# The first MLP's first matrix product by seven products of half size, with its results kept in DRAM until the second product

## The reference, cut to what matters

```python
def _rmsnorm(x, gain):
    y = xf * lax.rsqrt(jnp.mean(xf * xf, axis=-1, keepdims=True) + NORM_EPS)
    return (y * gain).astype(x.dtype)

def _squared_relu_mlp(h, w1, w2):          # w1: 1024 x 4096, w2: 4096 x 1024
    a = jax.nn.relu(h @ w1)
    return (a * a) @ w2

x = x + mix                                # mix = o @ w_out
x = x + _squared_relu_mlp(_rmsnorm(x, norm_mlp[layer]), mlp_w1[layer], mlp_w2[layer])
```

## Time and profile before

| | |
|---|---|
| median of three runs | 2844.92 us (2844.15 to 2849.19) |
| the profiled execution | 2845.62 us, span of its instructions 2843.8 us |
| TensorE busy | 2764.9 us, 97% of the span |
| VectorE, ScalarE busy | 1307.6 us, 890.9 us |
| DMA | 213 MB, 75 GB/s over the span |

### The profile page before, as it was taken

One profiled execution on the slowest core, in us unless ns is written; L12 is line 12 of the kernel. 1 busy time (PEld: TensorE's weight loads), 2 busy tenths in 40 slices (PEclk: granted clock), 3 DMA queues, 4 the chain that ended last, 5 costly groups with the idle time before them and its releaser, 6 DMA issues.

```text
span 2843.8 us, 40766 instructions
## 1 busy us (share of the span) xinstructions
PE 2764.9 (97%) x17644; PEld 2306.9 (81%) x17644; DVE 1307.6 (46%) x1649; ACT 890.9 (31%) x1304; POOL 177.1 (6%) x153
## 2 busy tenths in 40 slices
PE   8999998999999999998899999999999999999999
PEld 7887887878888888886889778877777888888887
DVE  6445454455444544336525555565635333333332
ACT  5445444331221111226222443344423111221111
POOL 2212122100000000005100000000000000000000
PEclk9999999999999999999899999999999999999999
DMA  4111110314333342122323221121711111111111
GB/s 130 41 36 31 38 39 24 110 61 133 113 111 125 126 126 74 45 67 75 114 89 103 66 78 50 49 70 36 283 52 45 45 52 45 52 46 51 51 46 67
DMA packets 211267, 213.08 MB, mean 75 GB/s; under 512 B 6929, under 2 KB 186641, under 8 KB 211089
## 3 DMA queue, kind: packets, MB, share of 16 engines
q1 hardware_dynamic: 211088, 210.48, 23.3%
HBM read 188.44 MB, written 22.02 MB: 74 GB/s over the span
## 4 chain that ended last, share of the span: by engine, by line
PE 75%; DVE 3%; ACT 3%; issue 1%; POOL 1%; DMA 0%; ACTq 0%; POOLq 0%; DVEq 0%; SPq 0%
PE ps L415 10%; PE ps L418 10%; PE ps L431 10%; PE ps L688 8%; PE ps L681 8%; PE ps L679 8%; PE ps L874 2%; PE ps L875 2%; PE ps L879 2%; PE ps L501 2%; PE ps L497 2%; PE ps L499 2%; PE ps L849 1%; PE ps L828 1%; ACT Whi L1125 1%
## 5 line engine op out<-in xcount | busy, mean ns | idle before, releaser
L1589 DVE TENSOR_TENSOR Wlo<-Wraw,Whi 128x1024 fp32r<-128x1024 f32 x216 | 268.7, 1249 | 946.7 <-ACT Whi L1125 946.7
L1125 ACT ACTIVATE Whi<-Wraw 128x1024 fp32r<-128x1024 f32 x228 | 239.6, 1057 | 1251.7 <-PE ps L431 573.6
L415 PE MATMUL ps<-Hh,Whi 128*128 128x512 f32 x1408 | 437.2, 392 | 0.0
L418 PE MATMUL ps<-Hh,Wlo 128*128 128x512 f32 x1408 | 434.5, 390 | 0.0
L679 PE MATMUL ps<-ah,Whi 128*128 128x512 f32 x1024 | 398.8, 389 | 1.2 <-ACT ah L1302 1.2
L681 PE MATMUL ps<-ah,Wlo 128*128 128x512 f32 x1024 | 398.4, 389 | 0.0
L431 PE MATMUL ps<-Hl,Whi 128*128 128x512 f32 x1392 | 339.2, 393 | 0.0
L418 PEld LDWEIGHTS ps<-Hh,Wlo 128*128 128x128 f32 x1408 | 264.8, 188 | 55.5
L415 PEld LDWEIGHTS ps<-Hh,Whi 128*128 128x128 f32 x1408 | 262.6, 188 | 53.8
L431 PEld LDWEIGHTS ps<-Hl,Whi 128*128 128x128 f32 x1392 | 259.5, 188 | 56.5 <-issue 3.3
L688 PE MATMUL ps<-al,Whi 128*128 128x512 f32 x1024 | 253.4, 389 | 0.1
(11 more groups left out here) (309 smaller groups left out, 3626.9 us busy)
## 6 DMA issues: line engine op xcount, KB each, us to landing
Wraw<-in_m_w SPq DMA_DIRECT2D x128, 512.0 KB, 4.0
n<-in_w_ada SPq DMA_DIRECT2D x64, 512.0 KB, 3.5
Wraw<-in_w_in SPq DMA_DIRECT2D x56, 512.0 KB, 4.1
R<-in_xT SPq DMA_DIRECT2D x16, 512.0 KB, 4.9
Wraw<-in_w_gate SPq DMA_DIRECT2D x16, 512.0 KB, 4.2
gate_scratch<-gr SPq DMA_DIRECT2D x32, 256.0 KB, 2.4
Wraw<-in_w_out SPq DMA_DIRECT2D x8, 512.0 KB, 4.3
xs_scratch<-R SPq DMA_DIRECT2D x8, 512.0 KB, 3.0
```

The lines of the kernel that those rows point to most:

```text
L415: e.matmul(t[:, c], wh[:, k, ms], opd.hi[:, k, c], start=k == 0, stop=False)
L418: e.matmul(t[:, c], wl[:, k, ms], opd.hi[:, k, c], start=False, stop=False)
L1125: e.activation(Whi[n % 4][:], Wraw[n % 2][:], ACT.Copy).then_inc(*S("w_hi").tick(n))
L1589: e.tensor_tensor(Wlo[n % 4][:], Wraw[n % 2][:], Whi[n % 4][:].bitcast(F), ALU.subtract).then_inc(*S("w_lo", "v").tick(n))
```

## The change

The first product (hidden = w1 transposed x) is cut in two in each of its three dimensions and made by Strassen's scheme in seven products of half blocks instead of eight. The hidden tiles go in 16 pairs q; a product takes 128 hidden rows, 4 pieces of width and 512 tokens: 12 matmuls. VectorE makes the sums of weight blocks (`a_sum`) and, once, the sums of x blocks (`b_minus`); both are split into high and low (`a_part`, `b_part`). `SEQ` gives the order of the 112 products. Partial sums stay in PSUM while further products are added to them, and ScalarE copies them out between (`part_copy`); VectorE adds what the four quarters of a pair need (`quarter`).

The operand is x times the gain, without the norm's root; the root (`rstd`) multiplies the results after ReLU. The last output tile of w_out is made in another order, so that its operands' buffers come free piece by piece.

The results are squared by ScalarE, written to DRAM (`a_scratch`) in quarters of 256 KB and read back as tiles of 512 KB (`a_load`) to 14 pairs of buffers, then split (`a_split`). All 32 hidden tiles are made before the first chunk. During chunk i SyncE loads the four tiles of chunk i + 1, one at each odd output tile.

The dot products all move into the second product: ten in each of the chunks 0 to 6 until they are used up, two at output tiles 0 and 4 and one at the others. In SyncE's program their loads now stand ahead of the weight's feed at each output tile; in VectorE's program they stay behind the addition.

The second MLP of the kernel is not changed.

```diff
+        a_d = nc.dram_tensor("a_scratch", [32, P, T], F, kind="Internal").ap()
...
-        WT += mlp_weights(m_w1, m_w2)
+        S2_0 = len(WT)
+        WT += [cols256(m_w2, 256 * j, 512 * i) for i in range(8) for j in range(4)]
...
+        SEQ = [(x, 0) for x in (1, 5, 6, 2, 7)]
+        for q in range(1, 16):
+            SEQ += [(1, q), (5, q), (4, q - 1), (6, q), (3, q - 1), (2, q), (7, q)]
+        SEQ += [(4, 15), (3, 15)]
...
+            def last_wout():
...
+                for k in range(8):
+                    pe.wait_ge(HO.hi_at(k), HO.lo_at(k))
+                    for hf, c in enumerate(HALF):
+                        e.matmul(t[:, c], wh[:, k, :], Hh[:, k, c], start=k == 0, stop=False)
+                        e.matmul(t[:, c], wl[:, k, :], Hh[:, k, c], start=False, stop=False)
+                        i = e.matmul(t[:, c], wh[:, k, :], Hl[:, k, c], start=False, stop=k == 7)
+                        if k == 7:
+                            full(i, b, occ, hf)
+                    if k < 7:
+                        i.then_inc(*S("wout_k").tick(k))
...
+            last_wout()
...
+            def product(s):
...
+                x, q = SEQ[s]
...
+                b, occ = PS["other" if x == 2 else "pair", q]
+                c = HALF[q % 2] if x == 2 else HALF[int(x in (3, 5))]
+                o, first = psum[b][:, c], x in (1, 2, 5)
...
+                pe.wait_ge(S("a_part_hi").at(s))
+                for k in range(4):
+                    pe.wait_ge(S("hi").at(b_hi(x, k)))
+                    e.matmul(o, h[:, k, :], Bh[x][:, k, :], start=first and k == 0, stop=False, skip_group_check=not first)
+                    pe.wait_ge(S("a_part_lo").at(s))
+                    e.matmul(o, l[:, k, :], Bh[x][:, k, :], start=False, stop=False, skip_group_check=not first)
+                    pe.wait_ge(S("lo", "v").at(b_lo(x, k)))
+                    i = e.matmul(o, h[:, k, :], Bl[x][:, k, :], start=False, stop=k == 3, skip_group_check=not first)
+                i.then_inc(*S("ps_full", b).tick(key))
...
+            for s in range(len(SEQ)):
+                if s == 2:
+                    rings["all"][1] = 2
+                    sums("mlp_norm", 3, 0, sq3[0], sq3[1])
+                product(s)
...
+            for c in range(8):
+                for jw in range(4):
+                    n, wh, wl = weight((0, "s2", c, jw), 4)
...
+                        for k in range(4):
+                            t = 4 * c + k
+                            pe.wait_ge(S("a_hi").at((0, t)))
+                            for cs in HALF:
+                                e.matmul(ps[:, cs], wh[:, k, ws], a_h[t % 14][:, cs], start=k == 0, stop=False)
+                            pe.wait_ge(lo_of(n))
+                            for cs in HALF:
+                                e.matmul(ps[:, cs], wl[:, k, ws], a_h[t % 14][:, cs], start=False, stop=False)
...
+            def pair_load(q):
...
+                    sp.wait_ge(S("a_part_hi").at(STEP[3, q - 2]), S("a_part_lo").at(STEP[3, q - 2]))
+                for x in range(2):
+                    e.dma_start(pair_raw[q % 2][:, 1024 * x:1024 * x + 1024].rearrange("p (a b) -> p a b", a=8),
+                                cols128(m_w1, 256 * q + 128 * x)).then_inc(*S("pair_raw", q % 2).tick((q, x), 16))
+            def quarter_out(s):
+                x, q = SEQ[s]
+                if x in QUARTER:
+                    n, t, hf = QUARTER[x]
+                    u = 4 * q + n
+                    sp.wait_ge(S("c_sq").at(u))
+                    e.dma_start(a_d[2 * q + t][:, HALF[hf]], ub[u % 3][:]).then_inc(*S("a_out", u % 3).tick(u, 16))
+            def a_load(t):
+                q = t // 2
+                for u in (4 * q + 1, 4 * q + 2) if t % 2 else (4 * q, 4 * q + 3):
+                    sp.wait_ge(S("a_out", u % 3).at(u))
+                if t >= 14:
+                    sp.wait_ge(full_at((0, "s2", (t - 14) // 4, 7)))
+                else:
+                    sp.wait_ge(product_full(STEP[LAST_USE[t], 15]))
+                if t >= 4:
+                    sp.wait_ge(S("a_hi").at((0, t - 4)))
+                e.dma_start(a_r[t % 14][:], a_d[t]).then_inc(*S("a_raw", t % 4).tick(t, 16))
...
+            pair_load(1)
+            for s in range(len(SEQ)):
+                x, q = SEQ[s]
+                if x == 4 and q + 2 < 16:
+                    pair_load(q + 2)
+                if s >= AHEAD:
+                    quarter_out(s - AHEAD)
+                if (x, q) == (4, 14):
+                    sp.wait_ge(S("a_part_hi").at(STEP[3, 14]), S("a_part_lo").at(STEP[3, 14]))
+                    feed(S2_0 + 2)
+                elif q == 15 and x in (2, 7):
+                    for t in range(2):
+                        a_load(2 * (x == 7) + t)
+            for s in range(len(SEQ) - AHEAD, len(SEQ)):
+                quarter_out(s)
...
                 if u == 0:
-                    sp.wait_ge(HM.lo_at(7), HM.lo_at(6))
+                    sp.wait_ge(S("c_scaled").at(63), *(S("a_out", u % 3).at(u) for u in (61, 62, 63)))
                 if j < 0:
...
                         sp.wait_ge(S("ada").at(u - 1))
...
                     e.dma_start((n3, n1)[u % 2][:], w_ada[j]).then_inc(*S("ada_raw", u % 2).tick(u, 16))
...
-            for kind, i in MLP:
-                if kind == "s1":
-                    feed(upto((0, "s1", i)))
-                    modulation()
-                    continue
+            for i in range(8):
                 for m in range(8):
+                    if i < 7:
+                        for _ in range(1 + (m % 4 == 0)):
+                            modulation()
                     if m % 2:
                         feed(upto((0, "s2", i, m // 2)))
-                    if i < 7:
-                        modulation()
...
-                    elif m == 0:
-                        while ada[0] < 66:
-                            modulation()
+                        if i < 7:
+                            a_load(4 * i + 4 + m // 2)
+                    if i == 7 and m == 0:
                         sp.wait_ge(full_at((0, "s2", 7, 0)))
...
+            def a_part(s):
+                x, q = SEQ[s]
+                act.wait_ge(ring_free(s), piece_at(x, q))
+                e.activation(Ah[s % 5][:], piece(x, q), ACT.Copy).then_inc(*S("a_part_hi").tick(s))
...
+            def part_copy(s):
...
+                act.wait_ge(product_full(s))
+                b, late = q % 2, q - (2 if x == 6 else 1)
+                if late >= 0:
+                    act.wait_ge(S("c_sum").at(4 * late + {1: 0, 6: 3, 7: 1}[x]))
+                e.activation({1: p1b, 6: wb[q % 2], 7: vb}[x][:], psum[b][:, HALF[0]], ACT.Copy).then_inc(
+                    *S("part_copy").tick(3 * q + (1, 6, 7).index(x)))
...
+            def squared(s):
+                x, q = SEQ[s]
+                if x in QUARTER:
+                    u = 4 * q + QUARTER[x][0]
+                    act.wait_ge(S("c_scaled").at(u))
+                    e.activation(ub[u % 3][:], ub[u % 3][:], ACT.Square).then_inc(*S("c_sq").tick(u))
...
+            def a_split(t):
+                act.wait_ge(S("a_raw", t % 4).at(t))
+                e.activation(a_h[t % 14][:], a_r[t % 14][:], ACT.Copy).then_inc(*S("a_hi").tick((0, t)))
...
+            for s in range(len(SEQ) + 2):
+                if s == 3:
+                    rstd("mlp_norm", 3, t2)
+                if 1 <= s <= len(SEQ):
+                    part_copy(s - 1)
+                if s + AHEAD < len(SEQ):
...
+            for i in range(8):
                 for m in range(8):
                     if m % 2:
                         feed(upto((0, "s2", i, m // 2)))
+                        if i < 7:
+                            a_split(4 * i + 4 + m // 2)
                     if i < 7:
-                        modulation()
+                        for _ in range(1 + (m % 4 == 0)):
+                            modulation()
                         continue
...
+            def a_sum(s):
...
+                x, q = SEQ[s]
+                r = pair_raw[q % 2]
+                if x == 5:
+                    dve.wait_ge(S("pair_raw", q % 2).at((q, 1)))
+                    if q:
+                        dve.wait_ge(S("a_part_hi").at(STEP[5, q - 1]), S("a_part_lo").at(STEP[5, q - 1]))
...
+                    i = e.tensor_tensor(Xs[:], r[:, 1024:1536], r[:, 1536:2048], ALU.add)
...
+            def a_part(s):
+                x, q = SEQ[s]
+                dve.wait_ge(S("a_part_hi").at(s), ring_free(s), piece_at(x, q))
+                e.tensor_tensor(Al[s % 5][:], piece(x, q), Ah[s % 5][:].bitcast(F), ALU.subtract).then_inc(
+                    *S("a_part_lo").tick(s))
...
+            def quarter(s):
...
+                x, q = SEQ[s]
+                if x not in QUARTER:
+                    return
+                n, t, hf = QUARTER[x]
+                u, c = 4 * q + n, HALF[hf]
+                o = ub[u % 3]
...
+                if x == 4:
```

(117 more changed lines are left out.)

313 lines of the change are left out of this document (245 added, 68 removed).

## The result

The changed kernel takes 2854.35 us (median of 7 executions, 2852.65 to 2857.86), the kernel before, timed beside it, 2845.64 (2844.15 to 2849.19). The ratio is 1.003, 95% interval 1.0018 to 1.0042: slower by 0.3%. The profiled execution has a span of 2852.5 us, 8.7 more than the earlier trace rows.

The account below looks back on a forecast made before the run. TensorE, busy 97% of 2843.8 us, was taken as the bound, with a queue-order loop taking over in the second stage. First product -43.5, entry -7.5 and second stage +63.9 gave +12.9, so 2858 us; range 2822 to 2884.

Parts of the forecast that it names:

- First product: First MLP product: 192 matmuls fewer at 0.2267 us, all added work hidden, 43.5 us less.
- a sign of being wrong: First product: gaps between products that wait for weight parts or copies of partial sums would show the prediction wrong.
- Entry: MLP entry: sums stay, operand scaling goes, 0.5 us of waits; 4.2 us instead of 11.7, 7.5 less.
- The loop: Second stage: loads behind a dot product's wait feed the next; turn 11.5 us, chunk 52.2, stage 63.9 more; chance 0.64.
- What binds in a turn: Second-stage turn: the result tile, third load, lands at 6.8 us and sets the turn; weights are converted by then.
- The late start: Second stage's start: dot product of tile 1 ends at 28.6 us instead of about 17; chunk 1's tile ready at 61.9.
- The clock: Chunk starts in the second stage: TensorE falls to 1.2 GHz after its stop, costing 1.4 us more a chunk.
- Sum: Whole kernel: -43.5 - 7.5 + 63.9 = +12.9 us, so 2858 against 2844.92.
- TensorE stays the bound: Rival, second stage: turn under 9.7 us and late start made up, only the gains left, 2794 us; chance 0.14.
- the loads of a train follow each other faster: Rival, second stage: third load lands at 6.1 us, turn 10.8, 16 us less, 2842; chance 0.08.
- the products slip: Rival, first product and entry: 1 us a pair and 4 at the entry add 20 us, 2878; chance 0.07.
- The rival of landings that grow with load: Rival, second stage: landings grow with DRAM load, turn 12.6 us, 25 us more, 2883; chance 0.07.

Follow-up runs that it names:

- Experiment 7: The changed kernel with weight and result-tile loads ahead of the dot products' loads, and ScalarE's copy ahead of the norm's root: 2794.66 us, 0.9816.
- experiment 1: The changed kernel with the weight's and result tile's loads both issued ahead of the dot product's load at odd output tiles: 2796.05 us, 0.9818.
- experiment 4: The changed kernel with a third buffer for the dot products' loads, SyncE's order as changed: 2799.66 us, 0.9839.
- experiment 3: The changed kernel with one dot product a tile in chunks 0 to 6, the ten left made at the head of chunk 7: 2849.41 us, 1.0006.
- experiment 5: The kernel before, with only the dot product's load put ahead of the weight's in the second product: 2845.9 us, 0.9997.
- Experiment 2: The changed kernel with only the result tile's load ahead of the dot product's load, the weight's behind: 2850.77 us, 1.0015.
- experiment 8: The changed kernel with only the weight's load ahead of the dot product's load, the result tile's behind: 2819.27 us, 0.9906.
- Experiment 6: The changed kernel with loads of weight pieces 2 and 3 of the second product ahead of the first dot product's load: 2851.97 us, 1.0025.

## Why the prediction came out as it did

The forecast was 2858, slower; measured are 2854.35, slower. By its steps:

- **First product, 43.5 less: right.** 192 matmuls fewer, 0.2267 us apart, clock 1.00, all added work hidden, but for two short waits. These waits for copies of partial sums were named as a sign of being wrong; they came, and are 2.6 us in all. First product and entry: 304.7 + 4.2 = 308.9 forecast, 311.3 measured.
- **Entry, 4.2 us: mis-sized by 2.4.** I looked for a weight part late at step 7 and gave it 0.5. What came was ScalarE's copy of a result behind the four instructions of the norm's root (1.69), and a copy late at the last products (0.91). Experiment 7 takes the first away, which shows it. ScalarE in the changed kernel, first and last instruction of the root and the copy:

```profile
608.88 0.67 ACT L1382 ACTIVATE t<-ps,eps 128x512 f32<-128x512 f32 x1
...
610.83 0.63 ACT L1384 ACTIVATE t<-t 128x512 f32<-128x512 f32 x1
611.36 0.58 ACT L1562 ACTIVATE wb<-ps 128x512 f32<-128x512 f32 x1
```

- **The loop: right by cause, and near by size.** The turn was forecast at 11.5 and measured at 11.3, 12.0 and 12.35 in chunk 0, and at 11.2 on average in the steady chunk, 11.0 where nothing stands between; the chunks at 52.2 and measured at 51.9, 50.7, 50.9, 53.9 and 52.3, the fourth with the second condition vector (forecast 54.6). Five and the vector add up to 259.6 against 263.4. Experiments 1 and 4 remove the loop in two ways and get 350.0 and 354.3 us for the stage. Experiments 3 and 5 show that it needs the new load.
- **What binds in a turn: half right.** I had the weights done by the time the tile lands. They are, but only by 0.2 us on ScalarE, and VectorE ends the weight's low part (942.79) when the tile's high part ends (942.81). Experiment 2 leaves the turn as it was with the tile's load taken away, experiment 8 shortens it to 9.8 with the weight's taken away: the weight was as much a bound as the tile.
- **The late start: right.** Dot product of tile 1 at 28.0 us against 28.6, first full wait ended at 62.5 against 61.9. Experiment 6 moves it by 3.1.
- **The clock: right.** The windows show mostly 1.2 GHz behind two of the stops, and all seven are followed by a pair of 1.22 us. TensorE's work between stops is 45.2 us (1021.54 to 1066.72) for 43.5. What a chunk loses by it is VectorE's wait at tile 0: 0.9 to 1.3 us, and 1.7 once. I had put 1.4, though the two numbers beside it (5.4 and 3.6) give up to 1.8.
- **Sum: +12.9 forecast, +8.7 measured.** Entry +2.4, second stage -2.2 (409.9 for 412.1), and -2.9 because the MLP before took 711.0 where the earlier trace rows add up to 708.1: 1.2 of it are two waits of 0.6 that I had left out, and the sum for the context's norm stands in it too. The last -1.5 lies behind the MLP, where the change touches nothing: from the MLP's end to the span's end the ten traces have 1534.6 to 1538.2 us (1537.0 before, 1535.5 after), so it lies within their scatter. In the range, the low end of 2822 is 3 us under what its three terms give (16, 9.5 and half of 15.7).

The rivals: that TensorE stays the bound is what experiment 1 makes of the kernel, and 2796 is what was worked out for it (2794); the change itself didn't do it. That the loads of a train follow each other faster (turn 10.8) came in part: the 11.2 of the steady chunk lie between its 10.8 and the 11.5 of the sum, and the five chunks came 3.8 us short of the forecast. The longer turns of chunk 0 (12.0 and 12.35) no run here explains. That the products slip fell, with 2.6 us in all. The rival of landings that grow with load fell: result tiles took 5.5 us at 189 GB/s. The rule named there, from the Trainium skill (DMA: Bandwidth & Descriptors, Latency and other measured facts), gives HBM's access 0.2 us on average and 2 us under high load. By it the same loads should have come later as the load rises. From 1000 to 1050 us the weights' and tiles' landings rose from 4.7 and 5.5 (189 GB/s) to 5.2 and 6.5 us (228 GB/s, experiment 1), in denser trains on one queue, and the dot products' fell from 3.9 to 3.6; so the trace gives no 1.8 us, and it can't tell latency from queueing in the rest.

## What to carry to other kernels

A load whose buffer is freed by a slow chain should stand in an in-order queue behind every load that this chain, or the bound engine, is waiting for; otherwise the chain waits for itself, and its turn, landing included, becomes the clock of the stage. To test such a loop, swap the order in the queue or add one buffer: here the one turned 0.3% slower into 1.8% faster, the other into 1.6%. When several loads stand behind the same wait, move them all: here the tile's load alone gave 3.6 us, the weight's alone 35, both together 58.

## What the runs showed of the hardware that was not expected

Three loads of 512 KB were issued within 1 us on one queue, and each was used behind the one before: conversions started 5.3 us (second load) and 6.6 us (third) after the release in the changed kernel, 5.4 for the second in experiment 2, and 5.2 in experiment 8 (from 1024.85 to 1030.01). In these runs the place in the train set the time and not what was loaded: as the second load, a result tile read back from DRAM in rows of 4 KB (5.2) was hardly faster than a weight (5.3 and 5.4). That short stops slow the first pair of matmuls less was not looked for either. The pair takes 0.61 at full clock, 0.73 to 0.74 us behind stops of 0.2 us (experiment 8, 1193.19) to 2.3 us (experiment 4, 1130.11), 1.09 behind one of 2.7 us (experiment 3, 1054.26), and 1.22 behind one of 4.1 us (experiment 8, 1146.88) and longer ones. What sets it these runs don't tell.
